# A two-layer trunk on eight cores: whole score blocks, decay tiles split by rows, the first keys moved into the last gates, roots in other PSUM banks, tap blocks on GpSimd's queue

## The chip, the cores and the metric

The kernel runs on the 8 cores of one Trainium2 chip. Each core computes one of the 8 sequences of the batch from its own copy of the inputs, and no core waits for another. The metric is the device time in microseconds (us) of the slowest core. A core has TensorE (PE, matrix products, which write to PSUM), VectorE (DVE), ScalarE (ACT, table functions), GpSimd (POOL) and SyncE (SP). POOL and SP issue the DMAs here, each from an in-order queue of its own.

## The reference

Two layers, each with two token mixers side by side, a gated MLP and an embedding gate. The change touches the mixers alone, mostly mixer A:

```
h = rmsnorm(x, g_mix[i]); proj = h @ w_in[i]
zq, zf, zi, zog, zglu, zga, zgb = jnp.split(proj, SPLITS, axis=-1)
# mixer A: gated recurrence S_t = diag(f_t) S_{t-1} + k_t v_t^T, o_t = S_t^T q_t, 4 heads of 128 x 128
o = hgrn2_recurrence(silu(zq), k_in, zi, log_f)
o = (rmsnorm(o, hg_norm_g[i]) * silu(zog)).astype(x.dtype)
y_a = o @ w_br_a[i]
# mixer B: GLU, causal depthwise convolution over 31 frames, layernorm, silu
u = (zglu + b_glu[i]); u = u[..., :512] * sigmoid(u[..., 512:])
u = silu(layernorm(causal_dwconv(u, conv_w[i], conv_b[i]), ln_g[i], ln_b[i]))
y_b = u @ w_br_b[i]
x = x + (sigmoid(zga) * y_a + sigmoid(zgb) * y_b) @ w_out[i]
```

x is (8, 2048, 1024), with 512 channels in each mixer.

## The kernel before

Channels lie on the 128 partitions and frames along the free dimension. A sequence is worked in two halves (`hf`) of 1024 frames, a half in two row blocks (`t_`) of 512. So `mixer(l, hf, W)` runs four times, and these are **the four passes** below: (layer 0, half 0), (0, 1), (1, 0), (1, 1). The program is written out in the order of the Python code: each engine has one list, and every instruction waits for the tiles that it reads and overwrites (`Prog.op`, class `Tl` keeps the last writer and the readers). No scheduler changes the order.

A pass has these stages.

- **Gates.** For each head (`hd`) and row block, `gate_mm` makes 8 matmuls each for forget (`f`), query, value and output gate, into one PSUM bank each from the ring that `set_banks` lays down. `gate_ev` reads the banks out, and `gate_ph2` makes the decays: `elc`, `emc` and `m` (three small tiles of `hsm_sb`, the decay at the end of a chunk, the one at its middle, and its logarithm), and the scaled `QT` and `KT` of 8 chunks of 128 frames. `closing` does the last two heads of the second row block. The first pass has an order of its own (`early`).
- **Fill and recurrence, woven.** `fill_steps` is mixer B: 16 GLU groups of 8 matmuls (a gate group, whose bank ACT reads with a Sigmoid, then a value group, whose bank DVE reads), 8 convolution steps of 18 matmuls (two tap blocks `g` of 9 lags each) and 4 steps of sums for the layernorm. `rec_steps` is mixer A, chunk by chunk: `keys(c)` transposes four key blocks into bank 0, lets ACT copy them to `Ktok`, makes the scores in bank 1, and DVE masks them into `smT`; `outer(c)` makes the outer products in bank 2, and four DVE operations renew the state and its bf16 copy `Sb2`; `rows(c)` makes the outputs in bank 3, which ACT squares (`osq_`) and DVE scales (`ot_`); `scale(c)` sums the squares of two chunks and takes the roots (Ln, then Exp on ACT); `rooted(c)` applies them. `n_side`, `n_main` and `lead` say after which fill step which recurrence step comes.
- **Scores.** They are causal, so the block of a head is made in two matmuls: all 128 keys against the later 64 queries, and the first 64 keys against the first 64 queries. DVE reads just these parts.
- **Tap blocks.** The convolution uses diagonal blocks of weights (128 x 1152, 288 KB) that the first pass builds and stores to DRAM (`scr_dg`). The other passes load them in `get_dg`, four in flight (`dgP`), on SP's queue, where `to_phases` also sends the GLU output out and back in another layout (`scr_u`).
- **Branches.** `ln_dve` and `ln_act` finish the layernorm (two DVE operations of 128 x 1024 per block, then four ACT operations of 128 x 256), `to_channels` sends the result through DRAM (`scr_n`) into `ucs`. `branch_a` needs no `ucs`; `branch_b` does, after its gate product. Both take pairs of banks in turn, 0-1, 2-3, 4-5, 6-7.

## Time and profile before

| | us |
|---|---|
| median of 3 runs, slowest core | 2245.28 (2244.7 to 2246.98) |
| the profiled execution's own time | 2240.89 |
| its span on the slowest core, core 1 (the others 2225.9 to 2237.3) | 2239.3 |
| TensorE busy in that span | 2083.4 |
| VectorE / ScalarE / GpSimd busy | 1403.8 / 1077.4 / 177.1 |

"Busy" of TensorE counts the time in which a matmul is under way, at whichever clock was granted. The granted clock is a share of full speed, 1.00 for 2.4 GHz and 0.50 for 1.2 GHz. A wait is shown as the idle time of an engine before an instruction, with the engine that ended it. Names of helpers hide what they are used for: nearly all matmuls have line 310, and the transposes of `keys` have line 861, so tiles and places in time tell them apart. `ps` is PSUM, `arena` the shared working memory, `ws_sb` the weight slots and `h_sb` the normalised input.

### The profile page before, as it was taken

How to read it: one execution, taken by the hardware profiler on the slowest of the kernel's cores; microseconds unless marked ns; L12 is line 12 of the kernel's file. 1: busy time of each engine (PE TensorE's matmuls, PEld its weight loads, DVE VectorE, ACT ScalarE, POOL GpSimd, SP SyncE). 2: the span in 40 equal slices, each digit the busy share in tenths (PEclk: the TensorE clock that was granted, in tenths of full speed). 3: DMA queues.
4: the chain of work that ended last, by engine and by line, in shares of the span. 5: the costliest groups of instructions: out<-in, count | busy, mean ns of one | idle time of the engine just before them, and what ended most of it. 6: DMA issues, size and time to landing. Idle time of an engine off the chain costs nothing.

```text
span 2239.3 us, 29208 instructions; the slowest of 8 cores (2225.9 to 2239.3 us)
## 1 busy us (share of the span) xinstructions
PE 2083.4 (93%) x10176; PEld 983.0 (44%) x10176; DVE 1403.8 (63%) x1861; ACT 1077.4 (48%) x1305; POOL 177.1 (8%) x190
## 2 busy tenths in 40 slices
PE   6988999889999999999898899989999999999985
PEld 1454444544444444444344644445444444444432
DVE  4686357554698349965667645575359852996257
ACT  3645155542677147722455532645247732874143
POOL 2120000000001000010000000000000010001000
PEclk8999999999999999999999999999999999999997
DMA  9946445365544665486446464356354366437434
GB/s 150 169 115 121 63 70 85 114 112 87 76 66 54 88 89 80 53 129 130 67 65 111 109 120 76 44 131 139 55 85 76 51 88 107 76 51 106 61 61 156
DMA packets 220854, 206.35 MB, mean 92 GB/s; under 512 B 19867, under 2 KB 195611, under 8 KB 220710
## 3 DMA queue, kind: packets, MB, share of 16 engines
q0 software_dynamic: 175520, 140.89, 44.2%
q1 hardware_dynamic: 45190, 63.59, 9.2%
q8 instruction: 84, 1.38, 0.3%
q14 instruction: 60, 0.49, 0.1%
HBM read 319.07 MB, written 26.26 MB: 154 GB/s over the span
## 4 chain that ended last, share of the span: by engine, by line
PE 78%; DVE 7%; ACT 7%; issue 4%; DMA 3%; SPq 1%; DVEq 0%; ACTq 0%; POOL 0%; POOLq 0%
PE ps L310 78%; ACT arena L319 5%; DVE arena L323 3%; DVE x_sb L323 1%; ACT L319 1%; DVE arena L327 1%; DMA ws_sb<-w_in 1%; DMA x_sb<-xT 1%; DMA arena<-scr_n 1%; DMA scr_u<-arena 0%; DMA arena<-scr_dg 0%; DVE arena L697 0%; DVE S L323 0%; SPq L774 0%; PE ps L861 0%
## 5 line engine op out<-in xcount | busy, mean ns | idle before, releaser
L310 PE MATMUL ps<-h_sb,ws_sb 128*128 128x512 bf16 x5376 | 1209.7, 383 | 33.4 <-ACT arena L319 16.3
L310 PEld LDWEIGHTS ps<-h_sb,ws_sb 128*128 128x128 bf16 x5376 | 526.3, 99 | 680.1 <-issue 71.4
L310 PE MATMUL ps<-arena,ws_sb 128*128 128x512 bf16 x2816 | 641.7, 383 | 21.5 <-ACT arena L319 10.3
L319 ACT ACTIVATE arena<-ps 128x1024 bf16<-128x1024 f32 (+3 forms) x484 | 400.7, 844 | 375.4 <-PE ps L310 358.4
L327 DVE SCALAR_TENSOR_TENSOR arena<-arena,cv_sb 128x1024 f32<-128x1024 bf16 x352 | 432.1, 1279 | 42.3 <-ACT arena L319 40.8
L310 PEld LDWEIGHTS ps<-arena,ws_sb 128*128 128x128 bf16 x2816 | 276.8, 99 | 362.9 <-issue 40.1
L319 ACT ACTIVATE arena<-x_sb 128x1024 bf16<-128x1024 f32 (+1 forms) x120 | 114.7, 969 | 474.1 <-DVE x_sb L323 364.6
L319 ACT ACTIVATE arena<-ps,cv_sb 128x1024 f32<-128x1024 f32 (+2 forms) x272 | 263.6, 971 | 121.2 <-PE ps L310 93.9
L323 DVE TENSOR_TENSOR arena<-arena 128x1024 bf16<-128x1024 f32 (+3 forms) x252 | 247.3, 1002 | 11.9 <-ACT arena L319 6.6
L319 ACT ACTIVATE arena<-arena 128x512 f32<-128x512 f32 (+3 forms) x256 | 203.2, 811 | 31.6 <-DVE arena L327 13.8
L327 DVE SCALAR_TENSOR_TENSOR arena<-arena,ps 128x1024 f32<-128x1024 f32 x64 | 77.8, 1221 | 188.1 <-PE ps L310 167.5
L310 PE MATMUL ps<-arena 128*128 128x256 bf16 (+2 forms) x1216 | 145.9, 258 | 31.0 <-ACT arena L319 10.3
L323 DVE TENSOR_TENSOR x_sb<-ps,x_sb 128x1024 f32<-128x1024 f32 x32 | 38.9, 1223 | 191.9 <-PE ps L310 191.9
L319 ACT ACT_TABLE_LOAD x75 | 96.2, 1283 | 98.3 <-PE ps L310 87.5
L310 PEld LDWEIGHTS ps<-arena 128*128 128x128 bf16 x1216 | 112.2, 104 | 66.3 <-issue 35.4
L310 PE MATMUL ps<-arena,ones 128*128 128x512 bf16 (+1 forms) x384 | 95.1, 351 | 34.8 <-ACT arena L319 30.6
L327 DVE SCALAR_TENSOR_TENSOR h_sb<-x_sb,cv_sb,arena 128x512 bf16<-128x512 f32 x160 | 111.0, 744 | 14.3 <-DMA arena<-scr_rs 8.5
L370 POOL DMA_DIRECT2D ws_sb<-w_up x48 | 42.0, 876 | 616.5 <-PE ps L310 616.5
L327 DVE SCALAR_TENSOR_TENSOR arena<-ps,cv_sb,arena 128x512 bf16<-128x512 f32 (+1 forms) x64 | 58.9, 932 | 44.8 <-ACT arena L319 33.5
L370 POOL DMA_DIRECT2D ws_sb<-w_in x36 | 32.4, 901 | 659.3 <-PE ps L310 610.9
L323 DVE TENSOR_TENSOR arena<-arena,ps 128x1024 f32<-128x1024 f32 x32 | 39.1, 1221 | 64.9 <-ACT arena L319 64.0
L327 DVE SCALAR_TENSOR_TENSOR x_sb<-ps,x_sb 128x1024 f32<-128x1024 f32 x32 | 38.8, 1222 | 52.5 <-PE ps L310 52.4
(56 smaller groups left out, 698.7 us busy)
## 6 DMA issues: line engine op xcount, KB each, us to landing
ws_sb<-w_up POOLq DMA_DIRECT2D x40, 1024.0 KB, 11.1
ws_sb<-w_in POOLq DMA_DIRECT2D x37, 1024.0 KB, 13.0
ws_sb<-w_down POOLq DMA_DIRECT2D x32, 704.0 KB, 8.5
arena<-scr_dg SPq DMA_DIRECT2D x48, 288.0 KB, 3.1
scr_dg<-arena SPq DMA_DIRECT2D x32, 288.0 KB, 3.5
x_sb<-xT SPq DMA_DIRECT2D x32, 256.0 KB, 8.2
ws_sb<-w_out POOLq DMA_DIRECT2D x8, 1024.0 KB, 11.7
ws_sb<-w_ple_gate POOLq DMA_DIRECT2D x8, 1024.0 KB, 11.6
```

The costliest lines, as they stand in the source:

```text
L310: P.op("pe", lambda e: e.matmul(out_ap, l_ap, r_ap, start=start, stop=stop), reads=[l_t, r_t], writes=[out_t], inc=inc)
L319: P.op("act", lambda e: e.activation(out=out_ap, in_=in_ap, func=func, **kw), reads=[in_t] + list(rd), writes=[out_t])
L323: P.op(eng, lambda e: e.tensor_tensor(out=out_ap, in0=a_ap, in1=b_ap, op=op), reads=[a_t, b_t], writes=[out_t])
L327: P.op("dve", lambda e: e.scalar_tensor_tensor(out=out_ap, in0=a_ap, scalar=scalar, in1=b_ap, op0=op0, op1=op1), reads=[a_t, b_t] + list(r ...
L370: return e.dma_start(out=sap[:, 0:k * ncol].rearrange("p (k n) -> p k n", k=k), in_=src[l, :, c0:c0 + ncol].rearrange("(k p) n -> p k n", ...
```

## The change

It has seven parts.

1. A score block is one matmul of 128 keys by 128 queries. The part that DVE does not read is made too, and not used.
2. `elc`, `emc` and `m` are two tiles each, one per row block, over the same memory.
3. `rec_steps` is made ahead of the gates, and in the passes other than the first, `closing` runs its first step (the state's scaling and `keys(0)`) right after the two forget groups. For this the ring of `closing` begins at bank 2 and has banks 0 and 1 last, so the two output-gate groups come into banks 0 and 1 behind `keys(0)`.
4. In these three passes the other 28 recurrence steps start one fill step later (`lead` 5 for 4), and end one step earlier (`tail` 1).
5. `scale` sums its second chunk in bank 3 (that of `rows`), not in bank 0 (that of the transposes), and does both Ln before both Exp.
6. Tap blocks are loaded from POOL's queue.
7. `branch_a(0, 0)` comes after two of the four `ln_dve` and ahead of the first `ln_act`, and `branch_a(0, 1)` between the second and third `ln_act`.

```
-        elc = Tl(hsm_sb[:, 0, :], "elc")
-        emc = Tl(hsm_sb[:, 1, :], "emc")
-        mm_ = Tl(hsm_sb[:, 2, :], "m")
+        elc_ = [Tl(hsm_sb[:, 0, :], "elc%d" % i) for i in range(2)]
+        emc_ = [Tl(hsm_sb[:, 1, :], "emc%d" % i) for i in range(2)]
+        mm2_ = [Tl(hsm_sb[:, 2, :], "m%d" % i) for i in range(2)]
...
             def closing(u0, u1, names):
                 pt = {}
+                if not early:
+                    set_banks((2, 3, 4, 5, 6, 7, 0, 1), ())
                 for nm in ("f", "q", "v", "og"):
                     for u in (u0, u1):
                         pt[u, nm] = gate_mm(u[0], u[1], nm) if nm in names else None
                     wrel(W[nm])
+                    if nm == "f" and not early:
+                        next(rec)
...
                 else:
-                    P.dma("sp", lambda e: e.dma_start(out=d.ap, in_=dg_t[l][g].ap), out_t=d, in_t=dg_t[l][g])
+                    P.dma("pool", lambda e: e.dma_start(out=d.ap, in_=dg_t[l][g].ap), out_t=d, in_t=dg_t[l][g])
...
                     for hd in range(4):
-                        b0 = hd * 128
-                        mm(p_sc, p_sc.ap[:, b0 + 64:b0 + 128], KT[c], KT[c].ap[:, b0:b0 + 128], QT[c], QT[c].ap[:, b0 + 64:b0 + 128],
-                           True, True, False)
-                        mm(p_sc, p_sc.ap[0:64, b0:b0 + 64], KT[c], KT[c].ap[:, b0:b0 + 64], QT[c], QT[c].ap[:, b0:b0 + 64],
-                           True, True, hd == 3)
+                        hs = slice(hd * 128, (hd + 1) * 128)
+                        mm(p_sc, p_sc.ap[:, hs], KT[c], KT[c].ap[:, hs], QT[c], QT[c].ap[:, hs], True, True, hd == 3)
...
                 def scale(c):
-                    for i in range(2):
-                        p_, o_ = (p_ss, p_tr)[i], osd[i]
-                        mm(p_, p_.ap, ones, ones.ap, osq_[i], osq_[i].ap, True, True, True)
-                        act(o_, o_.ap, p_, p_.ap, AF.Ln, bias=EPS, scale=1.0 / 128)
-                        act(o_, o_.ap, o_, o_.ap, AF.Exp, scale=-0.5)
+                    for p_, q_ in ((p_ss, osq_[0]), (p_o, osq_[1])):
+                        mm(p_, p_.ap, ones, ones.ap, q_, q_.ap, True, True, True)
+                    for p_, o_ in ((p_ss, osd[0]), (p_o, osd[1])):
+                        act(o_, o_.ap, p_, p_.ap, AF.Ln, bias=EPS, scale=1.0 / 128)
+                    for o_ in osd:
+                        act(o_, o_.ap, o_, o_.ap, AF.Exp, scale=-0.5)
...
-            n_side = 29
+            n_side = 29 if early else 28
             n_main = 28
-            lead = 4
+            lead, tail = (4, 0) if early else (5, 1)
             done = 0
             for i, _ in enumerate(fill_steps()):
-                while done * (n_main - lead) < (i + 1 - lead) * n_side:
+                while done < n_side and done * (n_main - lead - tail) < (i + 1 - lead) * n_side:
...
-            for cc in range(4):
-                ln_dve(cc)
+            ln_dve(0)
+            ln_dve(1)
+            branch_a(0, 0)
             ln_act(0)
+            ln_dve(2)
+            ln_dve(3)
             ln_act(1)
-            branch_a(0, 0)
+            branch_a(0, 1)
             ln_act(2)
             ln_act(3)
             to_channels()
-            for oi in range(1, 4):
-                branch_a(0, oi)
+            branch_a(0, 2)
+            branch_a(0, 3)
```

The order on TensorE, third pass, from the last gates on. The rows with `ws_sb,h_sb` are the value gates, the transposes with `ident` are those of `keys`. Before:

```order
L310 MATMUL ps<-ws_sb,h_sb 128x512 x16
L310 MATMUL ps<-h_sb,ws_sb 128x512 x56
L861 MATMUL ps<-ident,arena 128x128 x4
L310 MATMUL ps<-arena 128x64
L310 MATMUL ps<-arena 64x64
```

The same place now:

```order
L726 MATMUL ps<-ident,arena 128x128 x4
L310 MATMUL ps<-arena 128x128 x4
L310 MATMUL ps<-h_sb,ws_sb 128x512 x16
L310 MATMUL ps<-ws_sb,h_sb 128x512 x16
L310 MATMUL ps<-h_sb,ws_sb 128x512 x64
L310 MATMUL ps<-arena 128x128 x4
L726 MATMUL ps<-ident,arena 128x128 x4
L310 MATMUL ps<-arena 128x128 x4
```

Before, two output-gate groups and five fill groups (x56) stand behind the value gates and then come `keys(0)`, with two kinds of score matmuls in turn (four of each), and `outer(0)`. Now `keys(0)` stands ahead of the query gates, and after two output-gate groups and six fill groups (x64) come `outer(0)` and `keys(1)` at once.

The order on ScalarE around one `scale`, third pass. Banks are two to a `ps`: `ps0` is banks 0 and 1, `ps1` banks 2 and 3, `ps2` banks 4 and 5. Before:

```order
L319 ACTIVATE arena<-ps2 128x512
L319 ACTIVATE arena<-arena 128x512
L319 ACTIVATE arena<-ps0 128x512
L319 ACTIVATE arena<-arena 128x512
L319 ACTIVATE arena<-ps0 128x512
```

Now:

```order
L319 ACTIVATE arena<-ps2 128x512
L319 ACTIVATE arena<-ps1 128x512
L319 ACTIVATE arena<-arena 128x512 x2
L319 ACTIVATE arena<-ps0 128x512
L319 ACTIVATE arena<-ps2,cv_sb 128x512
```

The two roots are the first four operations, and the read of `ps0` behind them is the copy of the next transposes. The second sum now lies with the rows (`ps1`).

The order on the DMA queues, third pass. SP's, before:

```order
L772 DMA scr_u<-arena 128x1024
L774 DMA arena<-scr_u 32x4x256 x4
L769 DMA arena<-scr_dg_2 128x1152
L769 DMA arena<-scr_dg_3 128x1152
L772 DMA scr_u<-arena 128x1024
L774 DMA arena<-scr_u 32x4x256 x4
L769 DMA arena<-scr_dg_4 128x1152
L769 DMA arena<-scr_dg_5 128x1152
```

POOL's, now:

```order
L376 DMA ws_sb<-w_br_a 128x4x512
L380 DMA ws_sb<-w_br_b 128x4x512
L852 DMA arena<-scr_dg_0 128x1152
L852 DMA arena<-scr_dg_1 128x1152
L852 DMA arena<-scr_dg_2 128x1152
```

The 16 tap loads have left SP's queue, where the fifth stood behind the last pair of `scr_u` transfers, and stand on POOL's between the branch weights of the closing gates and the next two weight blocks.

## Rows read from the trace of the kernel before

**Rows 1.** The page, part 1: busy us (share of the span), instructions.

```profile
PE 2083.4 (93%) x10176; PEld 983.0 (44%) x10176; DVE 1403.8 (63%) x1861; ACT 1077.4 (48%) x1305; POOL 177.1 (8%) x190
```

**Rows 2.** Windows, the four passes, keys(0) to last sums: stretch, us, busy, clock, DMA.

```profile
109.60:188.00 78.40, 62.80 (x469) 41.90 (x468) 63.60 (x87) 37.32 (x62) 17.84 (x9) 0.93 0.37 106
377.60:453.70 76.10, 63.48 (x469) 41.95 (x468) 47.55 (x81) 39.18 (x65) 1.26 (x2) 0.91 0.47 115
1202.70:1279.40 76.70, 65.23 (x469) 42.80 (x468) 48.92 (x88) 40.32 (x66) 1.25 (x2) 0.89 0.45 114
1461.80:1538.20 76.40, 63.91 (x470) 42.40 (x469) 48.90 (x84) 40.32 (x66) 1.28 (x2) 0.91 0.44 114
```

**Rows 3.** Timeline of TensorE, third pass: start, length, instructions, [idle before <-releaser].

```profile
1207.83 0.38 PE L310 MATMUL ps<-arena 128*128 128x128 bf16 x4 [3.70 <-ACT arena L319]
1208.05 3.42 PE L310 MATMUL ps<-h_sb,ws_sb 128*128 128x512 bf16 x8
...
1211.68 1.19 PE L310 MATMUL ps<-arena 128*128 128x64 bf16 x8
1212.80 1.90 PE L310 MATMUL ps<-h_sb,ws_sb 128*128 128x512 bf16 x8
...
1216.71 0.39 PE L310 MATMUL ps<-arena 128*128 128x128 bf16 x4
1216.93 1.89 PE L310 MATMUL ps<-h_sb,ws_sb 128*128 128x512 bf16 x8
```

**Rows 4.** Waits of TensorE, whole program: us, times, longest.

```profile
PE ps L861 <- ACT arena L319: 16.9, 12, 2.0
PE ps L310 <- DMA arena<-scr_dg: 4.9, 2, 3.0
PE ps L310 <- DVE uhalo L339: 4.3, 1, 4.3
```

**Rows 5.** Timeline of ACT, then of DVE, third pass, at the first fill groups.

```profile
1203.22 1.28 ACT L319 ACT_TABLE_LOAD   x1
1204.51 1.26 ACT L319 ACTIVATE arena<-ps,cv_sb 128x512 f32<-128x512 f32 x2
1207.09 0.59 ACT L319 ACTIVATE arena<-ps 128x512 bf16<-128x512 bf16 x1
...
1205.30 2.33 DVE L327 SCALAR_TENSOR_TENSOR arena<-ps,cv_sb,arena 128x512 bf16<-128x512 f32 x2 [0.85 <-ACT arena L319]
```

**Rows 6.** Timeline of ACT, then of TensorE, third pass, at the first roots.

```profile
1227.73 0.58 ACT L319 ACTIVATE arena<-ps 128x512 f32<-128x512 f32 x1
...
1228.45 0.38 PE L861 MATMUL ps<-ident,arena 128*128 128x128 bf16 x4 [2.00 <-ACT arena L319]
```

**Rows 7.** SP's queue, third pass; then landing times of tap loads (SP), w_ple_proj (POOL).

```profile
1243.70 0.32 SPq L772 DMA_DIRECT2D scr_u<-arena  x1
...
1247.93 16.65 SPq L769 DMA_DIRECT2D arena<-scr_dg  x12
...
DMA to landing us min/median/max: 2.7/3.1/5.1
...
DMA to landing us min/median/max: 3.8/5.7/7.9
...
ws_sb<-w_ple_proj POOLq DMA_DIRECT2D x2, 256.0 KB, 3.8
```

**Rows 8.** Timeline of PE, ACT and SP, third pass, sums and branches.

```profile
1278.56 3.61 PE L310 MATMUL ps<-h_sb,ws_sb 128*128 128x512 bf16 x16 [1.01 <-ACT arena L319]
1279.04 0.37 ACT L319 ACTIVATE arena<-ps 128x256 f32<-128x256 f32 x1
1291.37 3.61 PE L310 MATMUL ps<-h_sb,ws_sb 128*128 128x512 bf16 x16 [2.29 <-ACT arena L319]
1298.58 1.91 SPq L963 DMA_DIRECT2D arena<-scr_n  x4
1306.10 1.89 PE L310 MATMUL ps<-arena,ws_sb 128*128 128x512 bf16 x8
```

More of the change, by code:

```diff
@@ L672, in mixer @@
             tmp = [[AR(57344 + (s * 5 + i) * 2048, 2048, F32, "tmp%d_%d" % (s, i)) for i in range(5)] for s in range(2)]
-            elc3 = elc.ap.rearrange("p (h c) -> p h c", h=4)
-            emc3 = emc.ap.rearrange("p (h c) -> p h c", h=4)
-            m3 = mm_.ap.rearrange("p (h c) -> p h c", h=4)
+            elc3, emc3, m3 = [hsm_sb[:, i, :].rearrange("p (h c) -> p h c", h=4) for i in range(3)]
             if hf == 0:
@@ L694, in gate_ph2 @@
                 cs = slice(t_ * 4, (t_ + 1) * 4)
+                elc, emc, mm_ = elc_[t_], emc_[t_], mm2_[t_]
                 four = lambda t: t.ap.rearrange("p (c t) -> p c t", c=4)
@@ L717, in closing @@
+            rec = rec_steps()
             def closing(u0, u1, names):
                 pt = {}
+                if not early:
+                    set_banks((2, 3, 4, 5, 6, 7, 0, 1), ())
                 for nm in ("f", "q", "v", "og"):
@@ L931, in mixer @@
-            rec = rec_steps()
-            n_side = 29
+            n_side = 29 if early else 28
             n_main = 28
-            lead = 4
+            lead, tail = (4, 0) if early else (5, 1)
             done = 0
             for i, _ in enumerate(fill_steps()):
-                while done * (n_main - lead) < (i + 1 - lead) * n_side:
+                while done < n_side and done * (n_main - lead - tail) < (i + 1 - lead) * n_side:
                     next(rec, None)
```

124 lines of the change are left out of this document (62 added, 62 removed).

## The prediction, made before the changed kernel had run

> **What bounds the kernel now.** I read the busy shares first: TensorE is busy 2083.4 of 2239.3 us and the next engine, VectorE, 1403.8 [rows 1]. So TensorE sets the time, and a change pays where TensorE is idle, where it works at the slow clock, or where it does work that it need not. The second view is a table of windows, one for each mixer pass, from keys(0) to the copy of the layernorm's means [rows 2]. There TensorE is idle 15.6, 12.6, 11.5 and 12.5 us (stretch less busy), and the mean granted clock is 0.93, 0.91, 0.89 and 0.91 where most of the program has 1.00. At the slow clock a matmul takes twice its time, so the clock costs (1 - clock) x stretch: 5.5, 6.8, 8.4 and 6.9 us. The third view, TensorE's timeline in the third pass, shows how the two hang together [rows 3]: after 3.70 us of waiting in front of outer(0), a group of 8 matmuls of 512 columns takes 3.42 us, and 1.90 later on. That is 1.2 GHz and then 2.4. The list of waits names the rest [rows 4]: transposes that wait for ACT (16.9 us, 12 times, at most 2.00), and tap loads (4.9, twice).
>
> So I work out a pass as: idle before less idle after, clock loss before less clock loss after, and the work saved. The third pass is replayed with its own durations; the second and fourth have its order and nearly its rows. The first has another order.
>
> **Scores.** Eight score matmuls stand 1.12 us apart from what follows (1211.68 to 1212.80), while four 128-column ones take 0.22 (1216.71 to 1216.93) [rows 3]. Whole blocks are four of the latter kind: 0.90 us less a chunk, 7.2 a pass over 8 chunks. At worst each keeps the 0.14 of an old one (4 x 0.14 = 0.56), which leaves 4.5 a pass. I take 7.2, since outer(c), rows(c) and the transposes have the same 128 columns and all run at 0.055. VectorE reads the same parts as before.
>
> **Keys inside the gates, outer(0) one group later.** Before, ACT copies Ktok(0) only at 1207.09, behind the table load and the Sigmoids of the fill [rows 5]. Now the copy stands ahead of the last gates' read-outs and is done some 10 us early, as is the mask. It puts 0.6 us ahead of the gates on ACT, and the decays end about 0.3 later. The 3.70 us do not all go: outer(0) writes bank 2, which the first fill group filled and ACT frees after the table load (1203.22 + 0.3 + 1.28 + 0.69, so about 1205.6), and TensorE is there at 1204.9. Behind outer(0) and keys(1) the seventh fill group wants bank 5, freed by the second of VectorE's two reads (1205.30 and 2.33 long [rows 5], plus 0.3), at 1208.1; TensorE is there at 1206.4. So 3.70 us of waiting become 0.65 + 1.75, but TensorE is one fill group, one transpose set and one score set further. Queued behind the moved step on VectorE are the gates' read-outs: they wait for ACT's Tanh anyway, and the output gates find bank 1 masked about 0.2 us early. That cover is thin; without it, a few tenths a pass.
>
> **Roots in other banks.** Transposes of keys(3), keys(5) and keys(7) waited for the second Ln to free bank 0: 2.00, 2.00 and 0.57 us [rows 6, 4]. Now they do not, and their copy comes 0.0 to 0.1 us later. What waits instead is rows(c), one or two groups later. By the replay that is free the first time (the Ln end at 1222.2, rows(2) comes at 1223.2) and 0.95 us the second. The sums of squares now also wait for ot (VectorE's read of bank 3), 0.1 to 0.75.
>
> **Tap loads.** SP's queue held the fifth tap load until scr_u had gone out (1243.70) and come back; it left at 1247.93 [rows 7], which is behind the waits of 3.0 and 1.8 in the second and fourth pass [rows 4] and a clock loss there. On POOL's queue nothing is ahead of it but weight issues that are long done, and the first four loads leave as soon as the gate buffers are free. SP keeps scr_u and gets its loads back sooner. The price is the landing: 2.7 to 5.1, median 3.1, on SP; POOL's nearest in size (256 KB) 3.8 to 7.9 [rows 7]. The two at 3.8 are the last ones, with little beside them; here no weight stream runs beside. The replay gives a load about 4.1 us from the end of its buffer's last matmul to the first of the next use. I take 4.3 and so 0.2 us at each of 5 steps, 1 us a pass; the ends are 0 (3.8) and 5 x 3.8 = 19 (7.9).
>
> A rule speaks against this part. Nothing in a trace with taps on SP can show it: POOL's descriptors. The Trainium skill, "SBUF — State Buffer", section "SBUF: two separate sides", says that POOL writes the descriptors of its own DMAs in software and is locked out while VectorE runs a copy in its fast mode, so such a DMA waits for the end of that copy. The copies here (Sb2, 0.43 us, and ucb, 0.69) are short, so by it a load would come at most 0.7 us later, 3.5 us a pass more if it hit all five steps.
>
> **What is late next.** As TensorE moves up, VectorE has the same 48.9 us of work [rows 2] in a stretch some 18 us shorter, busy 83% of it, and the tail chains through ACT: four Identity operations, a Square of 1024, osq(6), then VectorE's ot(6), then rows(7). In the replay TensorE waits 0.65 and 1.75 (above), 0.25, 0.45 (outer(3), for ACT's copy behind the roots), 0.55, 0.95, 0.35, 0.25, 0.85 (outer(7)), 0.3, 2.0 (rows(7), for bank 3) and 0.95 around the last sums: 9.3 us in all, against 11.5. Of the clock I keep one slow window of 3.4 us, after the 1.75: 1.7. Slow matmuls in the tail cost nothing, since the layernorm's chain sets the time from there.
>
> Third pass: 11.5 - 9.3 + 8.4 - 1.7 + 7.2 = 16.1. Second: 12.6 - 9.3 + 6.8 - 1.7 + 7.2 = 15.6. Fourth: 12.5 - 9.3 + 6.9 - 1.7 + 7.2 = 15.6. Together 47.3. Less the 1 us of taps three times: 44.3.
>
> **Branches.** The waits of 1.01 and 2.29 [rows 8] and a smaller one behind them go: the first bank pair is free, and both Tanh stand ahead of half the Silus. But over 3 us of idling become little time, for branch_b(0, 0) needs ucs, which lands about 5.4 us after the last of its loads begins (1298.58 + 1.91, TensorE at 1306.10 [rows 8]). That chain is 26.7 us from the copy of the means (1279.41), and its work is the same. With the two earlier Tanh and one t1 inside and the gaps between Silus filled, I get 26.2: 0.5 gained a pass. TensorE is at that point 4 x 5.18 + 3.45 = 24.2 us after its own start, so it will wait some 2.6 us there, and half the time 2 us of slow clock follows: 1.0. Net -0.5, three times: -1.5. The first pass is the same within this.
>
> **First pass.** Its order stays. Up to the first convolutions TensorE is the late one: five score sets (4.5) and one root wait of 2.0, less 0.5. After that the tap builds on POOL and VectorE and their stores on SP lead (a wait of 4.3 for VectorE [rows 4]; VectorE busy 63.6 of 78.4 [rows 2]), and further savings hide. I take 6.0, between 3 and 9.
>
> **Splitting the decay tiles** costs and gives nothing alone: it lets keys(0) start without a wait for the second row block.
>
> **Sum.** 44.3 - 1.5 + 6.0 = 48.8. The profiled execution took 2240.89, so 2192.1. The median of the runs is 4.4 us above it: 2196.5, and I say 2196. After the mixers all stages are fed by TensorE and shift whole.
>
> **Rivals.**
>
> A. Chains take over. If VectorE and ACT in order do not keep up (VectorE at 83% leaves 10 us slack a pass), each pass keeps 5 to 9 us more of waits, 15 to 27 in all: 2211 to 2223. For it: the replay has no jitter, and ten small waits each hang on it. Against: VectorE waits for ACT or PE in many places now.
>
> B. POOL's loads are slow, 6 us. Then each of 5 steps waits 1.7 more, and with a slow clock behind some, 10 a pass: 30, so 2226. For it: POOL's median in rows 7 is 5.7. Against: those loads cast, and ran beside weights. The rule on VectorE's lock would work this way: 3 x 3.5 = 10.5, so 2207. That is the section of the skill named above.
>
> C. The other side: POOL's loads take 7.9, as the slowest in rows 7. Each step then waits 3.6 more and runs at the slow clock after it (3.4 us, 1.7 lost): 5 x 5.3 = 27 a pass, 80 in all, 2277. It turns the change into a loss from a landing of about 6.5, where 5 x (2.2 + 1.2) x 3 = 51.
>
> D. More than forecast: no slow windows and replay waits half: 5 to 6 more a pass, 2178 to 2182.
>
> E. It does not do what it says: whole blocks keep 0.14 each. Then 2.7 of the 7.2 us are missing in each of 4 passes, 11 in all: 2207. It lies inside the forecast's own range.
>
> **How the numbers follow.** The forecast (2184 to 2210, with E and the rule on the lock) has 0.55, D 0.09, A 0.20, B 0.11, C 0.04, and 0.01 for no change. The range runs from 2180 to 2224: it takes in A and most of D and leaves out B's upper part and C. A measurement of this kernel can tell 0.2%, 4.5 us. Faster by more: all but C and no change, 0.95. Within: 0.01. Slower: 0.04.
>
> **What would show it.** Right: from outer(0) to the copy of the means some 56 to 58 us in the third pass, where it was 71.6 (1207.83 to 1279.4), a clock near 0.95 there, score sets of 4 x 0.055, no transpose waiting for ACT, no tap wait over 0.5, and new waits in front of the seventh fill group, rows(7) and branch_b(0, 0). Wrong: tap loads landing later than 5 us, transposes still waiting, or a clock in the passes still at 0.91; then the gain is half or less.

## The result: 0.6% faster, little more than a quarter of what was forecast

The changed kernel takes 2233.35 us (median of 5 runs) where the kernel before takes 2246.98 beside it: ratio 0.9938, with a 95% interval of 0.9919 to 0.9957. The forecast was 2196, between 2180 and 2224. So the sign was right, 14 us came where 49 were expected, and the time lies outside the range. The profiled execution took 2231.01 us, on its slowest core a span of 2229.6, against 2240.89 and 2239.3. One of the five executions took 2449.33 us, with half of the cores at a lower granted clock; the ratios here and below are of executions without that.

The page of the changed kernel, part 1, shows the riddle in one row. TensorE is busy 35.4 us less than in [rows 1], but the span is only 9.7 us shorter: 25.7 us of new idling.

```profile
PE 2048.0 (92%) x10048; PEld 960.6 (43%) x10048; DVE 1401.3 (63%) x1861; ACT 1073.0 (48%) x1305; POOL 202.9 (9%) x238
```

TensorE's waits in the changed kernel (us in total, times, longest), beside [rows 4]:

```profile
PE ps L310 <- ACT arena L319: 50.3, 28, 9.6
PE ps L310 <- DMA arena<-scr_n: 47.3, 4, 13.3
...
PE ps L310 <- DVE arena L327: 13.3, 11, 2.1
...
PE ps L310 <- DMA arena<-scr_dg: 4.8, 9, 1.4
```

The transposes that waited for ACT 12 times are gone from the list. In their place stands a wait of 47.3 us in four pieces for `arena<-scr_n`: the reads of `ucs`, one piece in each mixer pass, where the kernel before had 2.0 in two.

Where it sits is seen by cutting each pass in two. First, in both kernels, the stretch from outer(0) to the copy of the layernorm's means, for the second, third and fourth pass; then, for all four passes, the stretch from that copy to the first product that reads ucs in branch_b(0, 0). Columns: stretch, us, busy us of PE, PEld, DVE, ACT, POOL, clock, DMA share, GB/s. Windows of the kernel before:

```profile
381.58:453.70 72.12, 62.08 (x456) 40.96 (x457) 44.45 (x74) 36.16 (x60) 1.26 (x2) 0.91 0.44 113
1207.83:1279.40 71.57, 63.80 (x456) 41.79 (x457) 44.74 (x78) 36.10 (x60) 1.25 (x2) 0.88 0.40 110
1466.98:1538.20 71.22, 62.49 (x457) 41.39 (x458) 44.47 (x74) 36.11 (x60) 1.28 (x2) 0.90 0.38 107
188.00:215.10 27.10, 23.82 (x110) 10.37 (x109) 15.53 (x15) 15.59 (x25) 1.90 (x3) 1.00 0.91 163
453.70:481.50 27.80, 23.79 (x109) 10.31 (x107) 15.50 (x15) 16.18 (x24) 1.98 (x3) 1.00 0.86 166
1279.40:1306.10 26.70, 23.70 (x109) 10.37 (x108) 15.53 (x15) 15.16 (x24) 2.00 (x3) 1.00 0.88 175
1538.20:1564.20 26.00, 23.36 (x108) 10.30 (x107) 15.49 (x15) 15.15 (x23) 1.97 (x3) 1.00 0.92 181
```

The same windows of the changed kernel:

```profile
382.74:440.60 57.86, 50.38 (x419) 34.29 (x419) 45.27 (x72) 36.24 (x62) 8.35 (x16) 0.97 0.59 147
1205.07:1264.40 59.33, 52.58 (x419) 35.40 (x420) 45.39 (x76) 35.84 (x62) 8.35 (x16) 0.94 0.55 141
1460.18:1518.00 57.82, 49.52 (x419) 34.00 (x420) 44.89 (x72) 36.09 (x62) 8.57 (x16) 1.00 0.53 143
180.80:215.80 35.00, 22.70 (x107) 10.12 (x105) 15.47 (x15) 16.17 (x24) 2.54 (x4) 0.88 0.93 151
440.60:478.00 37.40, 24.12 (x113) 10.77 (x112) 15.06 (x15) 16.20 (x25) 3.28 (x4) 0.85 0.92 155
1264.40:1299.00 34.60, 23.75 (x111) 10.59 (x110) 15.45 (x15) 16.18 (x24) 3.28 (x4) 0.91 0.91 167
1518.00:1552.80 34.80, 23.91 (x112) 10.71 (x111) 15.49 (x15) 16.17 (x24) 3.28 (x4) 0.89 0.92 166
```

The recurrence does what was forecast: 72.1, 71.6 and 71.2 us became 57.9, 59.3 and 57.8, and in the first pass the copy of the means comes 7.2 us earlier (188.0 to 180.8). That is 14.2 + 12.3 + 13.4 + 7.2 = 47.1 us. Ahead of outer(0) there is some more, for its wait is shorter too. In the third pass the last group of 8 value gates that stands alone, before and now, is this:

```profile
1176.82 1.89 PE L310 MATMUL ps<-ws_sb,h_sb 128*128 128x512 bf16 x8
```

```profile
1176.10 1.89 PE L310 MATMUL ps<-ws_sb,h_sb 128*128 128x512 bf16 x8
```

From there to outer(0) it was 31.0 us (1207.83 less 1176.82) and is 29.0 (1205.07 less 1176.10). With the same in the second and fourth pass (31.1 to 29.0 and 31.1 to 29.4) that is 5.8 more, 52.9 in all.

Then the second stretch gives it back: 107.6 us in four passes became 141.8, so 34.2 us. TensorE's clock falls to 1.2 GHz in these waits, and stays there for 2.8 to 5.8 us after the work has resumed, which costs another 8.9 (half of 5.2, 5.8, 4.0 and 2.8). 43.1 of the 52.9 us are gone in one place of the program, and the 9.8 that are left are the 9.7 between the two spans. The window behind the wait in the third pass, with a clock of 0.50:

```profile
1299.00:1303.00 4.00, 4.00 (x10) 1.47 (x11) 0.32 (x1) 0.00 (x0) 0.00 (x0) 0.50 0.01 4
```

What happens there, in the third pass of the changed kernel: SP's queue, POOL's queue and TensorE.

```profile
1272.52 8.89 SPq L960 DMA_DIRECT2D scr_n<-arena  x4
1283.61 4.04 SPq L965 DMA_DIRECT2D arena<-scr_n  x4
...
1283.51 0.75 POOL L376 DMA_DIRECT2D ws_sb<-w_br_a  x1 [17.13 <-PE ps L310]
1284.25 0.75 POOL L380 DMA_DIRECT2D ws_sb<-w_br_b  x1
...
1299.00 3.57 PE L310 MATMUL ps<-arena,ws_sb 128*128 128x512 bf16 x8 [10.86 <-DMA arena<-scr_n]
```

Here the reads of ucs leave SP 19.3 us after the copy of the means (1264.35), as before (1298.58 [rows 8] less 1279.41 is 19.2). But at the same moment POOL issues two loads of 512 KB, `w_br_a` and `w_br_b`, the weights of the second branch block br1. They go into the slot of ga0, which is free once TensorE has finished branch_a(0, 3). In the third pass POOL's issue begins 0.1 us ahead of the first read, in the others 2.2, 2.7 and 1.7 us ahead. In the kernel before it was 3.0 us after the first read, and 2.8 to 3.0 in the others:

```profile
1301.58 0.75 POOL L376 DMA_DIRECT2D ws_sb<-w_br_a  x1 [21.66 <-PE ps L310]
```

Times from issue to landing of the 16 reads (minimum, median, maximum), first the kernel before, then the changed one:

```profile
L963 SPq DMA_DIRECT2D arena<-scr_n x16: 319/479/486, 207.1 to 1558.4; - x16
...
DMA to landing us min/median/max: 3.1/4.5/7.3
```

```profile
L965 SPq DMA_DIRECT2D arena<-scr_n x16: 319/844/3643, 201.2 to 1540.9; - x16
...
DMA to landing us min/median/max: 3.7/11.1/13.3
```

A read takes 11.1 us in place of 4.5, and even its issue on SP takes up to 3.6 us in place of 0.49. From the first issue to the last landing, the four reads of a pass took 7.7, 8.7, 7.3 and 6.9 us before, and 14.3, 15.0, 15.1 and 13.6 now, 27.4 us more in all. The rest of the 34.2, 6.8 us, is that the reads leave later after the copy of the means in three passes: 20.4, 22.1 and 20.9 us in the first, second and fourth, where it was 19.1, 18.9 and 18.8. They wait there for the last store of `scr_n`, which landed in 4.2, 4.7 and 3.7 us in place of 2.3, 2.1 and 2.0. So the theory after the result: **a weight load that used to leave behind the reads now leaves ahead of them, and they wait for it.** The rivals: the reads are slow for another reason (the two w_in blocks still landing, SP's queue), or the loss has to do with the faster recurrence as such.

### The profile page after: what moved, and what is told of

Same layout as the page of the kernel before. It is cut to its first block, busy times and chain, and to the rows that moved or that the text cites. A ratio compares the mean times of both kernels' runs of the same rounds, so it can differ in the third digit from the quotient of the medians.

```text
span 2229.6 us, 28952 instructions; the slowest of 8 cores (2221.6 to 2229.6 us)
## 1 busy us (share of the span) xinstructions
PE 2048.0 (92%) x10048; PEld 960.6 (43%) x10048; DVE 1401.3 (63%) x1861; ACT 1073.0 (48%) x1305; POOL 202.9 (9%) x238
## 4 chain that ended last, share of the span: by engine, by line
PE 76%; DVE 7%; ACT 6%; DMA 5%; issue 4%; SPq 1%; DVEq 0%; ACTq 0%; POOL 0%; POOLq 0%
PE ps L310 76%; ACT arena L319 5%; DVE arena L323 3%; DMA arena<-scr_n 2%; DVE x_sb L323 1%; DVE arena L327 1%; ACT L319 1%; DMA ws_sb<-w_in 1%; DMA arena<-scr_dg 1%; DMA x_sb<-xT 1%; DMA scr_n<-arena 1%; DVE S L323 1%; SPq L965 0%; DVE arena L696 0%; DVE x_sb L327 0%
## 5 line engine op out<-in xcount | busy, mean ns | idle before, releaser
L310 PE MATMUL ps<-arena,ws_sb 128*128 128x512 bf16 x2816 | 646.9, 385 | 67.7 <-DMA arena<-scr_n 47.3
L319 ACT ACTIVATE arena<-ps 128x1024 bf16<-128x1024 f32 (+4 forms) x484 | 399.5, 845 | 405.9 <-PE ps L310 398.8
L327 DVE SCALAR_TENSOR_TENSOR arena<-arena,cv_sb 128x1024 f32<-128x1024 bf16 x352 | 432.2, 1279 | 42.4 <-ACT arena L319 40.5
L327 DVE SCALAR_TENSOR_TENSOR arena<-arena,ps 128x1024 f32<-128x1024 f32 x64 | 78.1, 1220 | 231.5 <-PE ps L310 214.9
L310 PE MATMUL ps<-arena 128*128 128x256 bf16 (+1 forms) x1088 | 112.1, 253 | 31.7 <-DVE arena L327 8.0
L327 DVE SCALAR_TENSOR_TENSOR h_sb<-x_sb,cv_sb,arena 128x512 bf16<-128x512 f32 x160 | 111.0, 744 | 12.9 <-DMA arena<-scr_rs 7.0
L310 PEld LDWEIGHTS ps<-arena 128*128 128x128 bf16 x1088 | 88.9, 100 | 55.9 <-issue 42.0
L310 PEld LDWEIGHTS ps<-arena,ones 128*128 128x128 bf16 x384 | 37.1, 100 | 82.3 <-issue 57.9
L327 DVE SCALAR_TENSOR_TENSOR x_sb<-ps,x_sb 128x1024 f32<-128x1024 f32 x32 | 38.8, 1222 | 52.5 <-PE ps L310 52.4
## 6 DMA issues: line engine op xcount, KB each, us to landing
ws_sb<-w_up POOLq DMA_DIRECT2D x40, 1024.0 KB, 10.9
ws_sb<-w_ple_gate POOLq DMA_DIRECT2D x8, 1024.0 KB, 11.1
```

Of the source, the lines that this page charges most:

```text
L310: P.op("pe", lambda e: e.matmul(out_ap, l_ap, r_ap, start=start, stop=stop), reads=[l_t, r_t], writes=[out_t], inc=inc)
L319: P.op("act", lambda e: e.activation(out=out_ap, in_=in_ap, func=func, **kw), reads=[in_t] + list(rd), writes=[out_t])
L327: P.op("dve", lambda e: e.scalar_tensor_tensor(out=out_ap, in0=a_ap, scalar=scalar, in1=b_ap, op0=op0, op1=op1), reads=[a_t, b_t] + list(r ...
```

## Experiments

Twelve kernels, under nine heads. A ratio is always to the kernel before, run beside it on the same chip. Two of these kernels are compared by what each is below the kernel before.

**1. The load held back.** In the changed kernel the load of br1 waits until the reads have landed:

```diff
-                P.dmas([("pool", ...) for fn in blocks[i]], st)
+                P.dmas([("pool", ...) for fn in blocks[i]], st, wstate.get("ins", ()))
...
+            wstate["ins"] = [ucs]
             wrel(W["ga0"])
+            wstate["ins"] = ()
```

> The changed kernel, with one wait added: the load of the second branch weight block (w_br_a and w_br_b, 1 MB, issued by POOL as soon as TensorE has finished branch_a(0, 3)) waits until the four reads of ucs have landed. Theory 1 (that load goes ahead of the reads and holds them back): in the changed kernel the last read lands 15.1, 14.3, 15.0 and 13.6 us after the first is issued, in the kernel before 7.7, 8.7, 7.3 and 6.9. With the load held they take about 7.3 again, and TensorE waits at branch_b(0, 0) 5.4, 5.3, 2.7 and 4.4 us in place of 12.3, 13.3, 10.9 and 10.9: 29.5 us less, and some 5 us less of slow clock behind the waits. Time 2198, between 2190 and 2208. Theory 2 (the reads are slow for another reason, such as the two w_in blocks that are still landing or SP's slow issues): waits stay at 11 to 13 us and the time at 2233, within 4. Theory 3 (the held load comes too late itself): a new wait in front of branch_a(1, 0).

Ratio 0.9851 (0.9808 to 0.9894); three of the four executions are at 2203.31 to 2204.28, and one at 2226.91; I take their median, 2204, as its time. That one execution makes the interval 19 us wide, so that a difference of a few us to hold, in 7 and 8 below, is not clear of noise. TensorE's wait for the reads:

```profile
PE ps L310 <- DMA arena<-scr_n: 19.6, 4, 7.3
```

27.7 us of the wait are gone (29.5 expected), and some 26 us of the time, 40 us below the kernel before on that chip where the changed kernel was 14 below. The reads took 6.5, 8.4, 8.9 and 9.2 us, so theory 1 holds. The 2204 is above the 2198 that I gave: in the fourth pass a wait of 7.35 stays, since the last store of scr_n took 4.5 us to land where it took 2.0 before, and the reads 9.2 where they took 6.9. In the other passes that store took 3.3, 2.7 and 2.0 us, so the load of br1 was only a part of what held it up in the changed kernel; what the rest is, no run shows.

**2. The same wait in the kernel before,** as a control.

> The kernel before with the same wait as in the run hold. There the load of the second branch block is issued 1 to 3 us behind the first read already. Theory 1: only the second pass, whose reads took 8.7 us and made TensorE wait 1.40, gets a little faster: 2245, within 4 of the kernel before. The wait is worth something only in the changed kernel. If it were worth 10 us or more here, the gain in hold would not be owed to the collision that the change brought.

Ratio 1.0002 (0.9991 to 1.0013): worth nothing there, as theory 1 has it. The wait repairs only what the change broke.

**3. The collision alone, in the kernel before.** A 1 MB block is loaded a second time, just ahead of the reads:

```diff
+            fn, st = blocks[W["gb1"]][0], slots[W["gb1"] % NSLOT]
+            P.dmas([("pool", lambda e: fn(e, st.ap))], st, [un[3]])
             to_channels()
```

> The kernel before, with one load added in each mixer pass: the 1 MB weight block of gb1 is loaded a second time into the same place, by POOL, as soon as the last Silu is done, so just ahead of the four reads of ucs. Nothing else moves. Theory 1 (a weight load ahead of the reads costs them 7 us or so): the reads take 14 to 16 us from the first issue in place of 7 to 8.7, TensorE waits some 6 to 8 us at branch_b(0, 0) where it waited 0 to 1.4, and slow clock follows: 8 to 10 us a pass, 2280, between 2268 and 2290. Theory 2 (the reads' slowness in the changed kernel has another cause): the reads take 7 to 9 us and the time is 2246, within 4.

Ratio 1.0247 (1.0226 to 1.0267), 2299.65 us: 55 us slower, more than the 22 to 44 expected: the reads take 19.8 to 21.0 us. Probably br1's load comes on top, for it leaves 2.8 to 3.0 us behind the first read, when SP is still issuing the fourth; no run tells the two apart. TensorE, which waited 0 to 1.4 us there, now waits 12.4 to 13.9. Its row in the third pass stands behind SP's and POOL's:

```profile
1325.48 5.50 SPq L963 DMA_DIRECT2D arena<-scr_n  x4
...
1323.87 0.88 POOL L370 DMA_DIRECT2D ws_sb<-w_in  x1 [17.05 <-ACT arena L319]
...
1345.52 2.72 PE L310 MATMUL ps<-arena,ws_sb 128*128 128x512 bf16 x6 [12.40 <-DMA arena<-scr_n]
```

**4. Half of it.** hold, but `w_br_a` goes ahead as in the changed kernel and only `w_br_b` waits:

```diff
+                    P.dmas([("pool", ...) for fn in blocks[i][:1]], st)
+                    P.dmas([("pool", ...) for fn in blocks[i][1:]], st, ins)
```

> hold, but only the second half of the held load waits (w_br_b); w_br_a, 512 KB, goes ahead of the reads as in the changed kernel. Theory 1 (the reads are held back in proportion to the bytes that are queued ahead of them): their duration lies halfway, 11 us, TensorE waits some 8 us, and the time is 2204 + 4 x 3.7 = 2219, between 2212 and 2226. Theory 2 (any software-issued load ahead costs them the same): 2233. Theory 3 (only the bytes behind the first half count): 2204.

Ratio 0.9881 (0.9865 to 0.9896), 2218.36 us. With 0, 512 and 1024 KB ahead, the median time to land of a read is 4.8, 8.1 and 11.1 us, and TensorE waits 19.6, 28.4 and 47.3 us: some 3.2 us a read for each 512 KB. That is theory 1, although in the third pass w_br_a left 1.9 us behind the first read; there the reads took 11.1 us all the same, against 8.9 in hold. The landing times of the reads, in this run and then in hold:

```profile
DMA to landing us min/median/max: 4.1/8.1/11.9
```

```profile
DMA to landing us min/median/max: 3.0/4.8/7.8
```

**5. Which part of the change brings it.** The changed kernel with the old order of the branches, and nothing held:

```diff
-            ln_dve(0)
-            ln_dve(1)
-            branch_a(0, 0)
-            ln_act(0)
-            ln_dve(2)
-            ln_dve(3)
-            ln_act(1)
-            branch_a(0, 1)
+            for cc in range(4):
+                ln_dve(cc)
+            ln_act(0)
+            ln_act(1)
+            branch_a(0, 0)
             ln_act(2)
             ln_act(3)
             to_channels()
-            branch_a(0, 2)
-            branch_a(0, 3)
+            for oi in range(1, 4):
+                branch_a(0, oi)
```

> The changed kernel with one part undone, the order of the branches; no held load. In the kernel before, TensorE finishes branch_a(0, 3) 3.0 us after the first read of ucs is issued, in the changed kernel at the same time (both reads start 19.2 to 19.3 us behind the copy of the means). Theory 1 (the new order of the branches alone brings the collision, by taking 4 us of TensorE's waiting out of that stretch): the reads take about 8 us again, TensorE waits 1 to 5 us at branch_b(0, 0), and the time is that of hold_br (2200) or up to 8 above: 2204, between 2198 and 2212. Theory 2 (the faster recurrence brings it, so the order of the branches changes little): 2230, between 2225 and 2236.

Ratio 0.9853 (0.9835 to 0.987), 2214.44 us: undoing this one part makes the changed kernel some 19 us faster. It is 2 us above my bound, and the reason is in the trace. The old order makes TensorE later at branch_a(0, 3), and so the load, which leaves 2.05, 0.7, 2.5 and 1.4 us behind the first read. In the second pass that is between the second read and the third. SP's first two reads, POOL's load, and SP's last two, with their times to land:

```profile
L965 SPq DMA_DIRECT2D arena<-scr_n x2: 319/482/645, 454.7 to 455.1; - x2
...
DMA to landing us min/median/max: 3.4/3.9/4.5
```

```profile
455.42 0.76 POOL L376 DMA_DIRECT2D ws_sb<-w_br_a  x1 [20.06 <-PE ps L310]
```

```profile
L965 SPq DMA_DIRECT2D arena<-scr_n x2: 478/495/512, 455.8 to 456.3; - x2
...
DMA to landing us min/median/max: 11.3/12.8/14.2
```

Four equal reads, 0.4 to 0.7 us apart on one queue. The two that left ahead of the weight load took 3.4 and 4.5 us, the two behind it 11.3 and 14.2. No other row of this study shows the cause so plainly. The third pass shows that the start of an issue alone doesn't decide: the load left 1.1 us behind the start of the fourth read's issue, but that issue took 2.7 us, and the read landed in 11.4.

**6. That part alone, in the kernel before.**

```diff
-            for cc in range(4):
-                ln_dve(cc)
-            ...
+            ln_dve(0)
+            ln_dve(1)
+            branch_a(0, 0)
+            ...
```

> The kernel before with one part of the change alone, the new order of the branches. Theory 1: the 1 MB load goes ahead of the reads here too, the reads take 14 to 15 us, and TensorE waits 11 to 13 us at branch_b(0, 0) in place of 0 to 1.4, against 4 us of waits gone in front: 7.5 a pass and 2 of slow clock, 38 in all: 2280, between 2268 and 2292. Theory 2: 2243, within 4, as the prediction had it (0.5 a pass).

Ratio 1.012 (1.0101 to 1.0138), 2271.56 us: with the slow recurrence untouched, the new order of the branches costs 27 us. The reads took 13.4 to 16.1 us and TensorE waited 39.9 in four pieces. It is a part that looked worth 0.5 us a pass.

**7. Its worth without the collision.** hold with the old order of the branches (the diff is that of 5).

> hold, with the old order of the branches (all four ln_dve first, then ln_act(0), ln_act(1), branch_a(0, 0), and so on). Theory 1 (ucs sets the time of this stretch): the waits of 1.0, 2.3 and 0.7 at the branches come back and the wait at branch_b(0, 0) is 4 us shorter: same as hold within 3, 2201 to 2207. Theory 2 (the new order makes ucs itself earlier or later by more than 1 us a pass): a difference of 4 us or more.

Ratio 0.9804 (0.9788 to 0.982), 2200.26 us, some 4 us faster than hold, at the edge between the two theories: even without the collision the new order gains nothing that these runs can tell. TensorE's waits are moved in front of the branches, and its wait for the reads is 9.5 us in place of 19.6.

**8. What the rest of the change is worth.** Each of these undoes one part in hold, so that the collision doesn't cover it. Tap loads on SP's queue again:

```diff
-                    P.dma("pool", lambda e: e.dma_start(out=d.ap, in_=dg_t[l][g].ap), ...)
+                    P.dma("sp", lambda e: e.dma_start(out=d.ap, in_=dg_t[l][g].ap), ...)
```

> hold, with the tap loads back in SP's queue. Theory 1 (POOL's queue is worth something, as the prediction had it): the fifth and later tap loads stand behind the store and the four loads of scr_u; in the third pass they leave SP some 6 us later (1239.9 in place of 1233.55), so TensorE waits some 3.4 us and more at the slow clock behind it; 3 to 5 us a pass in three passes, 9 to 15 us slower than hold: 2207 to 2213. Theory 2 (the small waits for tap loads in the changed kernel, 4.8 us in all, are as large as what SP's order costs): same as hold within 3.

Ratio 0.9874 (0.9856 to 0.9893), 2213.53 us: 9 slower than hold, the lower end of what I gave. TensorE waits for taps 13.7 us in four pieces in place of 4.3 in seven. Its row where the fifth tap load was late, in the second pass:

```profile
413.51 1.86 PE L310 MATMUL ps<-arena 128*128 128x256 bf16 x8 [5.82 <-DMA arena<-scr_dg]
```

Scores in parts again:

```diff
-                    for hd in range(4):
-                        hs = slice(hd * 128, (hd + 1) * 128)
-                        mm(p_sc, p_sc.ap[:, hs], KT[c], KT[c].ap[:, hs], QT[c], QT[c].ap[:, hs], True, True, hd == 3)
+                    for hd in range(4):
+                        b0 = hd * 128
+                        mm(p_sc, p_sc.ap[:, b0 + 64:b0 + 128], ...)
+                        mm(p_sc, p_sc.ap[0:64, b0:b0 + 64], ...)
```

> hold, with the score products in parts again, as in the kernel before: eight matmuls a chunk instead of four whole blocks. Theory 1 (the prediction's term, 7.2 us a pass): 29 us slower than hold in four passes, 2233; between 2226 and 2238. Theory 2 (the prediction's rival E, 4.5 a pass): 18 slower, 2222. Theory 3 (TensorE reaches ucs later, so what is saved in the recurrence is mostly waited for at branch_b(0, 0)): the difference to hold is smaller by up to hold's waits there, 19.6 us in all: 2204 to 2214.

Ratio 0.9898 (0.9879 to 0.9918), from two executions, 2216.75 and 2222.86, so 26 and 20 below the kernel before where hold is 40 below: 14 to 20 us slower than hold, so between two of my theories. TensorE's busy time is the full term larger, 2084.5 against 2053.4 us in hold, 31.1 with the clock's share:

```profile
PE 2084.5 (94%) x10176; PEld 981.4 (44%) x10176; DVE 1403.2 (63%) x1861; ACT 1074.7 (48%) x1305; POOL 202.9 (9%) x238
```

But its idle time is 11.6 us less (137.0 of 2221.5 against 148.6 of 2202.0). So 31 us of work saved are 14 to 20 us of time; the rest turns into waits.

keys(0) back in the fill:

```diff
-                if not early:
-                    set_banks((2, 3, 4, 5, 6, 7, 0, 1), ())
...
-                    if nm == "f" and not early:
-                        next(rec)
...
-            n_side = 29 if early else 28
+            n_side = 29
-            lead, tail = (4, 0) if early else (5, 1)
+            lead, tail = 4, 0
```

> hold, with keys(0) back in the fill (at its fourth group, no bank order of its own in the last gates). Only the second, third and fourth pass change. Theory 1 (the prediction's replay): a wait of 3.7 in front of outer(0) in place of 0.7 and 1.7, and another 3.4 us of slow clock: 1.3 + 1.7 and about 1 for the later steps, 4 a pass, 12 in all: 2216. Theory 2 (the chains at the tail set the time anyway): within 4 of hold, 2200 to 2208.

Ratio 0.9836 (0.9819 to 0.9852), 2206.12 us, 37 below the kernel before: some 3 us slower than hold, which is theory 2 and within the noise. A wait of 4.5 to 4.6 us stands in front of outer(0) again in three passes, and TensorE waits 14.3 in place of 19.6 for the reads.

Sums of squares in banks 4 and 0 again:

```diff
-                    for p_, q_ in ((p_ss, osq_[0]), (p_o, osq_[1])):
-                        mm(p_, p_.ap, ones, ones.ap, q_, q_.ap, True, True, True)
-                    ...
+                    for i in range(2):
+                        p_, o_ = (p_ss, p_tr)[i], osd[i]
+                        mm(p_, p_.ap, ones, ones.ap, osq_[i], osq_[i].ap, True, True, True)
+                        ...
```

> hold, with the sums of squares back in banks 4 and 0, Ln and Exp one after the other for each. Theory 1 (the prediction's term): the transposes of keys(3), keys(5) and keys(7) wait 2.0, 2.0 and 0.6 again and the clock is slow behind them, 5 us a pass: 20 slower than hold, 2224, between 2214 and 2232. Theory 2 (the tail and ucs set the time, and the room in front of them takes the waits up, as it did for the keys): within 5 of hold, 2200 to 2209.

Ratio 0.9931 (0.9913 to 0.9949), 2230.1 us, 16 below the kernel before: 24 slower than hold, the dearest part to lose. The transposes' row of the waits (L726 is their line), and one transpose of the third pass that waits twice as long as any in [rows 4]:

```profile
PE ps L726 <- ACT arena L319: 25.9, 12, 4.0
```

```profile
1230.56 0.59 PE L726 MATMUL ps<-ident,arena 128*128 128x128 bf16 x4 [3.98 <-ACT arena L319]
```

**9. A version that beats both.** hold, with the gb product of branch_b(0, 1) ahead of the first product that reads ucs (branch_b is cut in two, front_b up to the Tanh and back_b behind it):

```diff
-            for oi in range(4):
+            fb = [front_b(0, oi) for oi in range(2)]
+            for oi in range(2):
+                back_b(0, oi, fb[oi])
+            for oi in range(2, 4):
                 branch_b(0, oi)
```

> hold, with the gb product of branch_b(0, 1) put ahead of the first product that reads ucs, so that TensorE has 3.45 us more of work while the four reads land. In hold TensorE waits 3.61, 4.39, 4.28 and 7.35 us there. Theory 1 (what is left of the wait is the length of the ucs chain alone): each wait gets 3.45 shorter, with some slow clock behind it gone too: 14 to 20 us faster than hold, whose undisturbed runs are at 2204: 2187, between 2183 and 2192. Theory 2 (TensorE's faster arrival only moves the waits on, to the pair swapped later or to the reads of the third pair): 2200 to 2204.

Ratio 0.9751 (0.9735 to 0.9767), 2186.83 us, 56 faster than the kernel before, and by the ratios 42 faster than the changed one. The wait for the reads has left the list altogether. In the third pass the last read lands at 1265.93, and TensorE begins at 1266.52 without a wait:

```profile
1259.35 7.34 PE L310 MATMUL ps<-h_sb,ws_sb 128*128 128x512 bf16 x32
1266.52 3.62 PE L310 MATMUL ps<-arena,ws_sb 128*128 128x512 bf16 x15
```

## Why the prediction was wrong, step by step

**What bounds the kernel, and the recurrence: right.** TensorE sets the time, its waits and its slow clock in the passes were the place to gain, and the sum for it came out: 44.3 for three passes and 6.0 for the first were forecast, and 45.7 (39.9 from outer(0) on and 5.8 ahead of it) and 7.2 measured. The sum is surer than its parts: undone one at a time in hold, scores, keys, roots and tap loads cost 14 to 20, 3, 24 and 9 us, where 29, 12, 20 and 9 to 15 had been expected of them.

- *Scores.* 7.2 a pass is right as work: the sets are 4 matmuls at 0.055, and undoing the part adds 31.1 us of busy time. As time it is 14 to 20 us of the 28.8 in the sum, a term that was too large by a third or more.
- *Keys inside the gates.* Forecast were waits of 0.65 and 1.75 in place of 3.70. Measured in the third pass:

```profile
1205.07 0.38 PE L310 MATMUL ps<-arena 128*128 128x128 bf16 x4 [0.73 <-ACT arena L319]
1205.29 0.39 PE L726 MATMUL ps<-ident,arena 128*128 128x128 bf16 x4
1205.51 0.39 PE L310 MATMUL ps<-arena 128*128 128x128 bf16 x4
1207.53 3.53 PE L310 MATMUL ps<-h_sb,ws_sb 128*128 128x512 bf16 x8 [1.63 <-DVE arena L327]
```

  0.73 and 1.63, and the group behind takes 3.53 us in place of 1.90: the clock is still slow there, as assumed. The part's worth was small, some 3 us in all, no more than the noise.
- *Roots.* The transposes no longer wait. Undone, the part costs 24 us, some 6 a pass.
- *Waits in the pass.* I gave 9.3 a pass and 1.7 for the clock. Measured (stretch less busy) 7.5, 6.8 and 8.3, and for the clock 1.7, 3.6 and 0. The stretch, forecast at 56 to 58 us, was 57.9, 59.3 and 57.8. Rival A, chains that take over, fell: VectorE was busy 45.3 of 57.9 us, and the waits in the passes came to no more than the forecast within a few tenths, though those on VectorE (`arena L327`) rose from 3.1 us in the whole program to 13.3.
- *Tap loads.* I took 4.3 us for a load on POOL's queue. The page of the profile shows a median of 4.2, and 4.8 us of waits in all where 3.0 were forecast:

```profile
arena<-scr_dg POOLq DMA_DIRECT2D x48, 288.0 KB, 4.2
```

  The longest of these waits is 1.4 us, where none over 0.5 was to be a sign of being right. The first four loads of each pass, which stand behind the branch weights on the queue, took 10.2 to 13.9 us, but TensorE waited for none of them; of the others none took over 5.5. So rivals B and C, slow loads, fell, and the move is worth some 9 us. POOL's issue took 537 ns in the median and at most 762, so POOL was never held up by more than 0.2 us there. The rule on the lock in the Trainium skill, "SBUF — State Buffer", section "SBUF: two separate sides", allowed 0.7 a load; no issue here shows it.

**The branches: the step that failed.** I gave this part -0.5 us a pass. Measured in four passes, the stretch from the copy of the means to the first product that reads ucs lost 34.2 us, and the clock behind it 8.9, together 43.1. Not all of that is this part's alone: by itself it costs 27 us in the kernel before (experiment 6), and undone in the changed one it gives back 19 (experiment 5), where holding the load gives 26 (experiment 1). The prediction put it so: "That chain is 26.7 us from the copy of the means, and its work is the same." The work is the same; what runs beside it is not. I worked out when TensorE would reach branch_b(0, 0), and found it 2.6 us early, but not what else TensorE releases on the way. Taking 4 us of waits out of branch_a brings the end of branch_a(0, 3) from 2.8 to 3.0 us behind the first read of ucs to 0.1 to 2.7 us ahead of it, and the 1 MB load of br1 with it. The row was to be had: POOL's queue in the kernel before, 1301.58, with a wait that TensorE ends, against SP's 1298.58 of [rows 8]. I weighed POOL's queue for the tap loads alone, and not for this stretch. From the first issue to the last landing I kept the 7.3 us of [rows 8]'s pass, where 14 to 15 was due, and 2.6 us of waiting became 10.9 to 13.3.

Two signs could have warned. [Rows 7] had a load of 5.7 and 7.9 us where weight streams ran beside, and I applied this to the taps (rivals B and C) but not to the reads. And in the second pass of the kernel before the reads took 8.7 us and not 7.3; the last of them, in flight beside br1's load, took 7.3 us where the first took 3.3.

What would have come with the collision avoided: 2204 in hold, against 2196 forecast. The 8 us between are about what TensorE waits at the reads beyond the forecast: 19.6 us, where I gave 2.6 a pass, 10.4.

How much of the slowing each of the two kinds of traffic causes isn't settled. The Trainium skill, "DMA: Bandwidth & Descriptors", section "Queues, rings and completion order", says that each DMA engine takes turns between the queues that it has work for, a packet at a time. By it a read next to a weight load gets a share and isn't shut out. The rows bear this out in part at most. In the third pass of the changed kernel the first read lands in 3.7 us, beside the load, but the other three land at 1295.1, 1296.5 and 1298.8, just as w_br_b lands (1295.21) or behind it; in the other passes even the first read lands between 0.6 us before w_br_b and 0.3 us behind it. And the delay grows with the bytes ahead. Why 1 MB has to land before the reads, of 256 KB each, do so isn't shown by the runs.

## What to carry to other kernels

When an edit makes an engine reach a point earlier, list everything that this point releases, on every queue: buffers that come free start loads, and a bulk load that passes a short transfer on the critical chain can hold it up, here by some 3 us for each 512 KB. Look for pairs in the trace, a DMA on the chain and a bulk DMA whose issue another engine ends, that lie within the time you mean to save; the remedy is to let the bulk load wait for the landing of the short one, and to put independent matmuls in front of the consumer. Price each part of a bundle where it stands: here the part that was put at 0.5 us a pass cost 27 us alone in the kernel before, and the place that it touched took back 43 of the 53 us that the passes had gained.

## What the runs showed of the hardware

- The order of issue of two queues can decide within a fraction of a microsecond: of four equal 256 KB reads on SP's queue, those issued 0.3 and 0.7 us before a 1 MB load of POOL's landed in 3.4 and 4.5 us, those 0.4 and 0.9 behind in 11.3 and 14.2. The edge isn't sharp. A read that left 0.1 us behind the start of POOL's issue landed in 3.7 us (third pass of the changed kernel), and one that left 1.1 us ahead of it, but whose own issue took 2.7 us, in 11.4 (third pass of experiment 5).
- SP itself is held up too: with that load ahead, an issue of a read took up to 3.6 us on SP's queue, 0.49 at most in the kernel before. With the load held, single issues still took up to 1.1 us in hold and 1.8 in hold_keys. What stood behind on that queue left later by as much.
- TensorE's granted clock was at 0.5 (1.2 GHz) from some point in each of the waits of 11 to 13 us, and for 2.8 to 5.8 us after work had resumed; so by an estimate (half of that time) such a wait costs 1.4 to 2.9 us more than its length.
- Work saved is not time saved where waits lie behind: 31 us less of matmuls in the recurrence gave 14 to 20 us.
